# Ten projection units of a float32-by-halves kernel computed as seven block products instead of eight

## The chip, the cores and the metric

One core of a Trainium2 chip. The metric is the device time of one launch in microseconds. The three runs of the kernel before gave 1618.77, 1618.77 and 1618.57 us; the median is 1618.77 us.

## The reference, cut to what matters

A first block (three gated branches) and then a second one (S5, convolution, gated linear attention), all in float32, on 512 tokens of 1024 features. The change touches only the first block:

```python
h = rmsnorm(x, norm_g[l])
proj = jnp.einsum('bsd,dn->bsn', h, w_in[l])          # 512x1024 by 1024x12288
a_u, a_v, a_z, b_p, b_z, c_h, c_b, c_c, c_z, gate_logits = jnp.split(proj, SPLIT_OFFSETS, axis=-1)
yc = c_b * causal_depthwise_conv(c_c * c_h, conv_w[l], conv_b[l]) * jax.nn.silu(c_z)   # three taps
gates = jax.nn.sigmoid(gate_logits.reshape(bsz, s, N_BRANCH, D_MODEL))
merged = (gates[:, :, 0] * (ya @ w_branch_a) + gates[:, :, 1] * (yb @ w_branch_b)
          + gates[:, :, 2] * (yc @ w_branch_c))
x = x + merged @ w_out[l]
```

`g2` below is the third gate, `w_b` and `w_c` are the products with `w_branch_b` and `w_branch_c`.

## The kernel before, in words

**A unit.** Every projection of 1024 output columns is a section of two units of 512 columns. The activations lie transposed in SBUF, features on partitions, in eight tiles of 128 x 512. Each float32 operand is held as a sum of two reduced parts, HH + HL for the activations and WH + WL for the weights, and a product is three matmuls, high by high, high by low and low by high (`halves`, line 2418). A unit is therefore 8 feature tiles x 4 column tiles x 3 = 96 matmuls of 128x128 by 128x512, into the four PSUM banks of one half of PSUM; the next unit uses the other half. All of them are issued at line 2471 (function `unit` of the PE block, called by `section`).

**Weights.** A unit's weights come as four chunks of 128 x 1024 (512 KB). SP loads a chunk into one of four slots of WR (lines 524 to 558) as soon as the chunk four before it has been split (`w_lo`); ScalarE copies it to WH (line 999, `split`), which waits until PE has finished with the chunk four before (`weights_used`); VectorE subtracts, WL = WR - WH (line 1570); PE then waits for `w_lo`. A chunk is 24 matmuls.

**Order.** There is no planner. `JOBS` (lines 72 to 133) lists the units and side jobs in PE's order with how many PSUM evictions ScalarE (`a`) and VectorE (`d`) make for each, and every semaphore value is counted from it. Each engine's program is written out by hand in that order. Around the change PE runs g1, c_h, w_b, c_c, g2, c_b, c_z, w_c, w_out. ScalarE evicts g1, c_h, g2 and c_z (lines 1037 and 1051, four instructions a unit). VectorE multiplies c_c from PSUM onto CH (line 1850), makes the three taps (lines 1855 and 1861), multiplies c_b from PSUM (line 1871), multiplies by silu(c_z) from TMP (line 1624), splits the branch outputs into YH and YL (line 1607) and merges (`merge`, lines 1829 and 1831). The residual X (2 MB) and the row FROW (512 KB) are loaded by SP after c_h (lines 630 and 631).

Of the kernel before, what the change touches and what calls it, by code (L numbers as in the profile page):

```python
# [14 lines left out]
F32 = mybir.dt.float32  # L15
# [22 lines left out]
T4 = 4  # L38
# [42 lines left out]

_add("params", side=1, a=2)
# [147 lines left out]
def three_branch_s5_gla_kernel(nc, a, out):  # L230
    ctx = ExitStack()
    with ctx:
# [31 lines left out]
        TMP = put("TMP", "TMP", [2, NC])  # L264

# [117 lines left out]
        def bank(name, m):  # L383
# [30 lines left out]
        pool_g, pool_w, pool_t = sem("pool_g"), sem("pool_w"), sem("pool_t")  # L414
        pool_rep = sem("pool_rep")
# [32 lines left out]
            "xg_half", "x_sums", "x_base", "x_left", "x_sum"))  # L448
        halves_done, y2_half, yg_done = sem("halves_done"), sem("y2_half"), sem("yg_done")
# [60 lines left out]
        def _(sp):  # L510
# [50 lines left out]

            def x_tile(t):
                sp.dma_start(X[:, t, :], x_d[:, t, :]).then_inc(x_in[t], 16)
# [41 lines left out]
            sp.wait_ge(pool_g, 1)  # L605
# [21 lines left out]
            section("c_h", w_in, W_IN["c_h"])  # L627
            sp.wait_ge(side_done, side_after("pool.1"))
            sp.wait_ge(s5_out, 16 * S5_OUT)
            sp.dma_start(X[:, :, :], x_d).then_inc(x_again, 16)  # L630
            sp.dma_start(FROW[:, :], a["final_g"].rearrange("(o n) -> o n", o=1).broadcast_to([P, D])).then_inc(frow_in, 16)
            section("w_b", a["w_branch_b"][0], 0)
            for name in ("c_c", "g2", "c_b", "c_z"):
                section(name, w_in, W_IN[name])
            section("w_c", a["w_branch_c"][0], 0)
# [121 lines left out]
        def _(pool):  # L757
# [104 lines left out]
            pool.memset(MJ8[:, 0, 0:1], 0.0).then_inc(pool_w, 1)  # L862
# [20 lines left out]
            pool.memset(MJ8[:, 0, 1:2], 0.0).then_inc(pool_g, 1)  # L883
# [12 lines left out]
            pool.tensor_tensor(TM[:, :, :], TM[:, :, :], DT2[:, :, :], ALU.add).then_inc(pool_t, 1)  # L896

            pool.wait_ge(side_done, side_after("w_t.1"))
            for ri in range(2):
                pool.tensor_copy(WST[:, ri, :, 0:T4 - 1, :],  # L900
                                 WST[:, ri, :, T4 - 1:T4, :].to_broadcast([P, PAIRS, T4 - 1, S5_GROUP])).then_inc(pool_rep, 1)
# [81 lines left out]
        def _(act):  # L983
# [9 lines left out]
            def split(count=4):  # L993
# [8 lines left out]
                state["chunk"] = min(state["chunk"] + count, N_STATIC)  # L1002

# [136 lines left out]
            act.wait_ge(pool_t, 1)  # L1140
# [45 lines left out]
            evac("g1.0", [G[:, m, :] for m in range(4)], ACT.Sigmoid)  # L1186
            split()
# [1750 lines left out]
```

## Time and profile before

| what | value |
|---|---|
| median of the runs (1618.57 to 1618.77) | 1618.77 us |
| span of the profiled execution | 1617.1 us |
| what the median has beyond that span | 1.7 us |
| granted TensorE clock over the span | 0.999 |
| PE busy | 1606.0 us, 99% |
| VectorE busy | 952.0 us, 59% |
| ScalarE busy | 667.2 us, 41% |
| HBM traffic | 128 GB/s |

The profiled execution has no total of its own beside its span, so the working goes by the span and the 1.7 us are carried along. PE's busy time is the union of matmuls whose ends are modelled, so the share alone does not tell at what rate they follow each other; the distance between their starts does.

### The profile page before, as it was taken

What the parts mean: (1) busy time and instruction counts of PE and PEld (TensorE: products, weight loads), DVE (VectorE), ACT (ScalarE), POOL (GpSimd) and SP (SyncE); (2) the same over time, 40 slices, a digit from 0 to 9 for tenths busy, and PEclk for the clock granted to TensorE, in tenths of its full rate; (3) what the DMA queues carried; (4) which work ended last, traced back from release to release, by engine and by line L of the source; (5) the groups of instructions that cost most, each with busy time, mean ns of one, the idle gap of its engine ahead of it and who ended that gap; (6) DMA issues with size and microseconds to landing.
All of it is one profiled execution on the core that took longest, in us unless ns stands there. A gap on an engine that the chain in (4) does not pass through costs nothing.

```text
span 1617.1 us, 19917 instructions
## 1 busy us (share of the span) xinstructions
PE 1606.0 (99%) x7833; PEld 1344.3 (83%) x7833; DVE 952.0 (59%) x1325; ACT 667.2 (41%) x936; POOL 204.3 (13%) x237
## 2 busy tenths in 40 slices
PE   9999999999999999999999999999999999999998
PEld 7888888888888888888898889887888888888887
DVE  5267274663235424456899999985473535455357
ACT  5333342253222223335455454558255425343254
POOL 4991000000000000001323221121000000000000
PEclk9999999999999999999999999999999999999999
DMA  8664643233433333332988988498623123122221
GB/s 243 172 171 135 164 118 93 76 93 103 157 96 98 95 103 92 102 93 80 314 166 204 189 194 220 105 205 182 194 72 93 66 90 106 54 77 91 79 77 66
DMA packets 152395, 207.41 MB, mean 128 GB/s; under 512 B 52289, under 2 KB 75509, under 8 KB 151670
## 3 DMA queue, kind: packets, MB, share of 16 engines
q1 hardware_dynamic: 133077, 174.22, 34.9%
q0 software_dynamic: 17568, 29.89, 11.1%
q10 hardware_dynamic: 1664, 2.13, 0.5%
q8 instruction: 58, 0.95, 0.2%
q14 instruction: 28, 0.22, 0.0%
HBM read 191.53 MB, written 14.68 MB: 128 GB/s over the span
## 4 chain that ended last, share of the span: by engine, by line
PE 97%; DVE 1%; ACT 1%; DMA 0%; issue 0%; DVEq 0%; SPq 0%; ACTq 0%
PE PS L2471 82%; PE PS L2449 3%; PE PS L2839 1%; PE PS L2548 1%; PE PS L2789 1%; PE PS L2691 1%; PE PS L2869 1%; PE PS L2658 1%; PE PS L2641 0%; PE PS L2845 0%; PE PS L2717 0%; PE PS L2626 0%; PE PS L2715 0%; PE PS L2716 0%; ACT XN L1006 0%; PE PS L2826 0%
## 5 line engine op out<-in xcount | busy, mean ns | idle before, releaser
L2471 PE MATMUL PS<-HH,WH 128*128 128x512 f32 x1216 | 474.7, 390 | 0.8 <-ACT G L1037 0.4
L2471 PE MATMUL PS<-HH,WL 128*128 128x512 f32 x1216 | 473.3, 389 | 0.0
L2471 PE MATMUL PS<-HL,WH 128*128 128x512 f32 x1216 | 473.2, 389 | 0.0
L999 ACT ACTIVATE WH<-WR 128x1024 fp32r<-128x1024 f32 x200 | 211.9, 1061 | 596.9 <-PE PS L2471 558.9
L1570 DVE TENSOR_TENSOR WL<-WR,WH 128x1024 fp32r<-128x1024 f32 x144 | 186.1, 1299 | 391.9 <-ACT WH L999 391.3
L2471 PEld LDWEIGHTS PS<-HH,WH 128*128 128x128 f32 x1216 | 228.3, 188 | 49.4 <-issue 2.1
L2471 PEld LDWEIGHTS PS<-HH,WL 128*128 128x128 f32 x1216 | 228.3, 188 | 47.8
L2471 PEld LDWEIGHTS PS<-HL,WH 128*128 128x128 f32 x1216 | 228.3, 188 | 47.0
L2022 DVE SCALAR_TENSOR_TENSOR TMP<-CP,PRM,TMP 128x512 f32<-128x512 f32 x232 | 155.0, 748 | 0.0
L2471 PE MATMUL PS<-WH,HH 128*128 128x512 f32 x320 | 126.8, 396 | 0.0
L2471 PE MATMUL PS<-WL,HH 128*128 128x512 f32 x320 | 125.1, 391 | 0.0
L2471 PE MATMUL PS<-WH,HL 128*128 128x512 f32 x320 | 125.1, 391 | 0.0
L2471 PE MATMUL PS<-YH,WH 128*128 128x512 f32 x320 | 124.6, 389 | 0.0
L2471 PE MATMUL PS<-YH,WL 128*128 128x512 f32 x320 | 124.5, 389 | 0.0
L2471 PE MATMUL PS<-YL,WH 128*128 128x512 f32 x320 | 124.5, 389 | 0.0
L1601 DVE TENSOR_TENSOR WL<-WR,WH 128x1024 fp32r<-128x1024 f32 x64 | 76.3, 1220 | 52.5 <-ACT WH L1025 52.5
L1025 ACT ACTIVATE WH<-WR 128x1024 fp32r<-128x1024 f32 x64 | 66.3, 1058 | 83.0 <-PE PS L2471 81.8
L2471 PEld LDWEIGHTS PS<-WH,HH 128*128 128x128 f32 x320 | 67.9, 212 | 13.1 <-issue 3.0
L2471 PEld LDWEIGHTS PS<-WH,HL 128*128 128x128 f32 x320 | 67.9, 212 | 10.5 <-issue 0.7
L2471 PEld LDWEIGHTS PS<-WL,HH 128*128 128x128 f32 x320 | 67.9, 212 | 10.1
L2471 PEld LDWEIGHTS PS<-YL,WH 128*128 128x128 f32 x320 | 60.1, 188 | 12.5
L2471 PEld LDWEIGHTS PS<-YH,WH 128*128 128x128 f32 x320 | 60.1, 188 | 12.5
(398 smaller groups left out, 2099.6 us busy)
## 6 DMA issues: line engine op xcount, KB each, us to landing
WR<-in_w_in_dram SPq DMA_DIRECT2D x96, 512.0 KB, 3.8
WR<-in_od_w_in_dram SPq DMA_DIRECT2D x32, 512.0 KB, 4.0
WR<-in_ev_w_in_dram SPq DMA_DIRECT2D x24, 512.0 KB, 4.6
WL<-in_ev_w_in_dram POOLq DMA_DIRECT2D x24, 512.0 KB, 7.6
WR<-in_ev_w_in_dram SPq DMA_DIRECT2D x32, 256.0 KB, 3.1
WR<-in_ev_w_out_dram SPq DMA_DIRECT2D x16, 512.0 KB, 5.3
WR<-in_od_w_in_dram SPq DMA_DIRECT2D x32, 256.0 KB, 3.4
WR<-in_od_w_out_dram SPq DMA_DIRECT2D x16, 512.0 KB, 3.8
```

What stands on the lines that cost most here:

```text
L999: act.activation(WH[:, n % RING, :, :], WR[:, n % RING, :, :], ACT.Copy).then_inc(w_hi, 1)
L1025: act.activation(WH[:, j % RING, :, :], WR[:, j % RING, :, :], ACT.Copy).then_inc(w_hi, 1)
L1570: dve.tensor_tensor(WL[:, s, :, :], WR[:, s, :, :], WH[:, s, :, :].bitcast(F32), ALU.subtract).then_inc(w_lo, SUM_TO - SUM_FROM + 1 if n = ...
L1601: dve.tensor_tensor(WL[:, s, :, :], WR[:, s, :, :], WH[:, s, :, :].bitcast(F32), ALU.subtract).then_inc(w_lo, 1)
L2022: o = dve.scalar_tensor_tensor(CP[:, kt, CPAD:] if last else TMP[:, s, :], CP[:, kt, k:k + SEQ], w, TMP[:, s, :], ALU.mult, ALU.add)
L2449: mm = pe.matmul(out_banks[m], tok(acts(kt)[ai], m), (WH, WL)[wi][:, q, kk, :], start=(kt == 0 and i == 0), stop=(kt == KT - 1 and i == 2))
L2471: mm = pe.matmul(out_banks[m], st, mv, start=(kt == 0 and i == 0), stop=(kt == 2 * per - 1 and i == 2))
L2548: mm = pe.matmul(bank("a_v.0", t), tile(H(2 * q + kk)[ai], t), (WH, WL)[wi][:, q, kk, :], start=(q == 0 and kk == 0 and i == 0), stop=(q = ...
L2658: mm = pe.matmul(bank(f"pool.{i}", m), (PWH, PWL)[wi][:, g, k, (kt % 2) * P:(kt % 2 + 1) * P], Y(2 * g + k)[ai], start=(k == 0 and j == 0) ...
L2691: mm = pe.matmul(bank(f"s5_z.{i}", m)[:, r * P:(r + 1) * P], WT[m // 2][:, pr, :], UT[:, pr, :], start=True, stop=True)
L2789: mm = pe.matmul(out_bank[:, cols], tile(acts(kt)[ai], t), (WH, WL)[wi][:, 2 * u + kt // 2, kt % 2, cols], start=(kt == 0 and i == 0), sto ...
L2839: mm = pe.matmul(A[m][:, s * P:SEQ], (V2, V2L)[wi][:, s, m * P:(m + 1) * P], scores, start=(s == 0 and i == 0), stop=(s == TT - 1 and i == ...
```

## The change

Ten units (c_h, c_c, c_b, c_z and g2, two each) are computed by a seven-product scheme for 2 x 2 blocks (features halved, columns halved, tokens halved). A block product is 4 feature tiles x 2 column tiles x 3 = 24 matmuls of 128x128 by 128x256, so a unit is 168 of them. The activation side needs four combinations of blocks (S1 to S4), made once ahead of c_h. The weight side needs four sums of blocks for each unit, made on VectorE in place in the raw buffer. There are seven operands instead of four chunks to split for each unit, and the results are put together in SBUF by two ScalarE and five VectorE instructions. The products with silu and sigmoid are applied in place afterwards. The units of c_h and c_c now stand together, w_b comes after them, then c_b, c_z and g2; the taps of c run on VectorE under c_c.1 and w_b, the other elementwise work of c under c_b.1 to g2.1. The loads of X and FROW move behind g2.1. Some semaphores of POOL's tables are put together in one.

```diff
+def _seven(name, ends=(0, 0)):
+    for u in range(2):
+        SEVEN.append(f"{name}.{u}")
+        _add(f"{name}.{u}", 7 + ends[u], 0, 2, 5)
...
-_section("c_h", a=4)
+_seven("c_h")
+_seven("c_c")
 _section("w_b", d=4)
-_section("c_c", d=4)
-_section("g2", a=4)
-_section("c_b", d=4)
-_section("c_z", a=4)
+_seven("c_b")
+_seven("c_z")
+_seven("g2", (0, 2))
 _section("w_c", d=4)
...
+BLOCK_AT = ((0, 0), (0, 1), (1, 1), (1, 0))
+OPERAND_AT = (0, 0, 0, 1, 3, 2, 3)
+OPERAND_SUM = {1: 1, 3: 2, 2: 3, 6: 4}
... SP
+                for place in (1, 0, 2, 3) if again else range(4):
+                    if again and place == 0:
+                        sp.wait_ge(sums_made, sums_after(j - 1))
+                    elif again:
+                        sp.wait_ge(w_lo, chunks_before(before) + (0, 4, 6, 7)[place])
+                    else:
+                        sp.wait_ge(w_lo, n0 - RING + place + 1)
+                    i, half = BLOCK_AT[place]
+                    c0 = W_IN[name] + int(u) * NC + half * (NC // 2)
+                    sp.dma_start(WRS[:, place, :, :], w_in[4 * P * i:4 * P * (i + 1), c0:c0 + NC // 2]
...
+            sp.wait_ge(weights_used, used_after("g2.1"))
             sp.dma_start(X[:, :, :], x_d).then_inc(x_again, 16)
             sp.dma_start(FROW[:, :], ...)
... ScalarE
+            def high(job, i):
+                n, j = chunks_before(job) + i, SEVEN.index(job)
+                if i in OPERAND_SUM:
+                    act.wait_ge(sums_made, sums_after(j, OPERAND_SUM[i]))
+                else:
+                    act.wait_ge(w_loaded[OPERAND_AT[i]], 16 * block_loads(job))
+                act.wait_ge(weights_used, n - RING + 1)
+                act.activation(WHS[:, n % RING, :, :], WRS[:, OPERAND_AT[i], :, :], ACT.Copy).then_inc(w_hi, ends)
+            def seven(job, to, following, func=ACT.Copy, skip=0, acted=None, between=None):
+                def finish(i, j, k):
+                    if acted:
+                        act.wait_ge(banks_dve, dve_after(job, k))
+                        act.activation(block_of(to, i, j, kt0, skip), block_of(to, i, j, kt0, skip), func).then_inc(acted, 1)
+                act.wait_ge(weights_used, n0 + 1)
+                act.activation(block_of(to, 1, 1, kt0, skip), paired(job, 0), ACT.Copy).then_inc(banks_act, 1)
+                for i in range(4, 7):
+                    high(job, i)
+                if between:
+                    between()
+                next_high(following, 0)
+                act.wait_ge(weights_used, n0 + 5)
+                act.activation(block_of(to, 0, 0, kt0, skip), paired(job, 0), func).then_inc(banks_act, 1)
+                next_high(following, 1)
+                finish(1, 1, 3)
+                next_high(following, 2)
+                finish(0, 1, 4)
+                next_high(following, 3)
+                finish(1, 0, 5)
...
+            for i in range(3):
+                high("c_h.0", i)
+            act.wait_ge(weights_used, used_after("g1.1"))
+            combination_hi(4, corner(HH, 1, 0), S3R[:, :, :])
... VectorE
+            def low(job, i):
+                dve.wait_ge(w_hi, n + 1)
+                dve.tensor_tensor(WLS[:, n % RING, :, :], WRS[:, OPERAND_AT[i], :, :], WHS[:, n % RING, :, :].bitcast(F32),
+                                  ALU.subtract).then_inc(w_lo, ends)
+            def block_sum(to, other):
+                dve.tensor_tensor(WRS[:, to, :, :], WRS[:, to, :, :], WRS[:, other, :, :], ALU.add).then_inc(sums_made, 1)
+            def next_low(job, i):
+                low(job, i)
+                if i == 0:
+                    dve.wait_ge(w_loaded[1], 16 * block_loads(job))
+                    block_sum(0, 1)
+                elif i == 1:
+                    dve.wait_ge(sums_made, sums_after(j, 1))
+                    block_sum(0, 2)
+            def next_outer(job):
+                if job in SEVEN:
+                    dve.wait_ge(w_loaded[2], 16 * block_loads(job))
+                    block_sum(1, 2)
+            def seven(job, to, following, work=iter(()), paces=(1, 0, 1, 0, 1, 1), skip=0):
+                low(job, 4)
+                dve.wait_ge(sums_made, sums_after(j, 3))
+                block_sum(3, 0)
+                others(paces[0])
+                low(job, 5)
+                others(paces[1])
+                dve.wait_ge(banks_act, act_after(job, 1))
+                dve.wait_ge(weights_used, n0 + 3)
+                dve.tensor_tensor(c21, c22, c, ALU.subtract).then_inc(banks_dve, 1)
+                dve.wait_ge(banks_dve, dve_after(job, 1))
+                dve.tensor_tensor(c22, c21, b, ALU.add).then_inc(banks_dve, 1)
+                low(job, 6)
+                others(paces[2])
+                dve.wait_ge(weights_used, n0 + 4)
+                dve.scalar_tensor_tensor(c22, c22, -1.0, d, ALU.mult, ALU.subtract).then_inc(banks_dve, 1)
+                others(paces[3])
+                next_low(following, 0)
+                next_outer(following)
+                next_low(following, 1)
+                others(paces[4])
+                dve.wait_ge(weights_used, n0 + 6)
+                dve.scalar_tensor_tensor(c12, c21, -1.0, b, ALU.mult, ALU.subtract).then_inc(banks_dve, 1)
+                next_low(following, 2)
+                dve.wait_ge(weights_used, n0 + 7)
+                dve.tensor_tensor(c21, c21, d, ALU.add).then_inc(banks_dve, 1)
+                next_low(following, 3)
+                others(paces[5])
...
+            seven("c_c.0", U, "c_c.1")
+            seven("c_c.1", U, "w_b.0", taps, (1, 1, 1, 1, 1, 1))
+            for _ in taps:
+                pass
+            taps = convolved(1)
+            for n in (5, 5, 6):
+                split(1)
+                for _ in range(n):
+                    next(taps)
...
+            seven("c_b.1", CH, "c_z.0", weighed(0), skip=PPAD)
+            seven("c_z.0", CH, "c_z.1", weighed(1), skip=PPAD)
+            seven("c_z.1", CH, "g2.0", gated_c(0), skip=PPAD)
+            seven("g2.0", G, "g2.1", gated_c(1))
+            seven("g2.1", G, "w_c.0", low_c(range(4)))
... PE
+            def seven(job):
+                for i, (m, x) in enumerate(zip((0, 1, 2, 3, 0, 1, 3), blocks)):
+                    low_ready(n)
+                    if i < 4:
+                        free_bank(job, m)
+                    elif i == 4:
+                        pe.wait_ge(banks_act, act_after(job, 1))
+                    else:
+                        pe.wait_ge(banks_dve, dve_after(job, i - 3))
+                    if job == SEVEN[0] and 1 <= i < 4:
+                        pe.wait_ge(parts_dve, COMBINED + (1, 2, 4)[i - 1])
+                    for kt in range(4):
+                        for half in range(2):
+                            out_cols = slice(half * (SEQ // 2), (half + 1) * (SEQ // 2))
+                            for j, (wi, ai) in enumerate(halves):
+                                mm = pe.matmul(bank(job, m)[:, out_cols], (WHS, WLS)[wi][:, n % RING, kt, half * P:(half + 1) * P],
+                                               x[ai][:, kt, :], start=..., stop=..., skip_group_check=True)
+                    mm.then_inc(weights_used, used_after(job) - n if i == 6 else 1)
```

The four combinations take ten VectorE instructions of 128 x 1024 ahead of `next_low("c_h.0", 0)` (S1: three, S2: two, S4: two, S3: three, each waiting for the one before), four ScalarE copies to high parts, and four VectorE subtractions to low parts; the fourth pair overwrites a corner of HH and HL, so it waits for the end of g1.1.

## Rows read from the trace of the kernel before

**Rows 1.** The page: engines' busy time, and the granted clock.
```profile
PE 1606.0 (99%) x7833; PEld 1344.3 (83%) x7833; DVE 952.0 (59%) x1325; ACT 667.2 (41%) x936; POOL 204.3 (13%) x237
...
PEclk9999999999999999999999999999999999999999
```
**Rows 2.** Busy time by stretch: PE, PEld, DVE, ACT, POOL, PEclk, DMA share, GB/s.
```profile
450.00:620.00 170.00, 170.00 (x751) 140.81 (x751) 70.59 (x87) 36.77 (x39) 0.00 (x0) 1.00 0.33 96
...
990.00:1014.00 24.00, 24.00 (x213) 23.85 (x212) 24.00 (x38) 11.39 (x18) 1.20 (x1) 1.00 0.87 263
```
**Rows 3.** Who waited for whom, 300 to 760 us.
```profile
ACT WH L999 <- PE PS L2471: 281.4, 72, 4.4
...
PEld PS L2519 <- DVE XN L1910: 0.3, 1, 0.3
```
**Rows 4.** Timeline of PE in a unit: first and last of 75 512-column matmuls.
```profile
1354.77 0.39 PE L2471 MATMUL PS<-HH,WH 128*128 128x512 f32 x1
...
1371.54 0.39 PE L2471 MATMUL PS<-HH,WL 128*128 128x512 f32 x1
```
**Rows 5.** Timeline near the end: first and last of 24 256-column matmuls, one load.
```profile
1608.56 0.28 PE L2789 MATMUL PS<-WH,OH 128*128 128x256 f32 x1
1608.57 0.19 PEld L2789 LDWEIGHTS PS<-WH,OL 128*128 128x128 f32 x1
...
1611.32 0.28 PE L2789 MATMUL PS<-WL,OH 128*128 128x256 f32 x1
```
**Rows 6.** Chain of waits: pairs of 128-column matmuls, each with its weight load.
```profile
991.27 0.22 PE PS L2716 x2
991.49 0.22 PE PS L2717 x2
```
**Rows 7.** Groups by line and shape, VectorE and ScalarE, 320 to 760 us.
```profile
L1570 DVE TENSOR_TENSOR WL<-WR,WH 128x1024 fp32r<-128x1024 f32 x79 | 96.3, 1224 | 224.6 <-ACT WH L999 224.6
...
L1829 DVE TENSOR_TENSOR TMP<-PS,G 128x512 f32<-128x512 f32 x16 | 10.9, 683 | 0.0
...
L999 ACT ACTIVATE WH<-WR 128x1024 fp32r<-128x1024 f32 x77 | 81.5, 1060 | 263.9 <-PE PS L2471 263.9
```
**Rows 8.** Timeline of VectorE: runs of instructions, and one that waits for another.
```profile
361.50 4.91 DVE L1607 TENSOR_TENSOR YL<-CH,YH 128x512 fp32r<-128x512 f32 x8
366.32 2.35 DVE L1570 TENSOR_TENSOR WL<-WR,WH 128x1024 fp32r<-128x1024 f32 x2
...
378.19 1.23 DVE L1570 TENSOR_TENSOR WL<-WR,WH 128x1024 fp32r<-128x1024 f32 x1 [4.21 <-ACT WH L999]
...
466.37 0.68 DVE L1829 TENSOR_TENSOR TMP<-PS,G 128x512 f32<-128x512 f32 x1
467.09 0.69 DVE L1831 TENSOR_TENSOR M<-M,TMP 128x512 f32<-128x512 f32 x1
...
514.11 5.38 DVE L1861 SCALAR_TENSOR_TENSOR U<-CH,PRM,U 128x512 f32<-128x512 f32 x8
```
**Rows 9.** Timeline of ScalarE: splits, a table load and an eviction around g1.
```profile
371.66 1.06 ACT L999 ACTIVATE WH<-WR 128x1024 fp32r<-128x1024 f32 x1 [4.38 <-PE PS L2471]
...
378.18 1.28 ACT L1037 ACT_TABLE_LOAD   x1
379.47 2.07 ACT L1037 ACTIVATE G<-PS 128x512 f32<-128x512 f32 x4
```
**Rows 10.** DMA issues: KB each, median us to landing.
```profile
WR<-in_w_in_dram SPq DMA_DIRECT2D x96, 512.0 KB, 3.8
...
WR<-in_ev_w_in_dram SPq DMA_DIRECT2D x32, 256.0 KB, 3.1
...
X<-in_x_dram SPq DMA_DIRECT2D x1, 2048.0 KB, 8.7
...
FROW<-in_final_g_dram SPq DMA_DIRECT2D x1, 512.0 KB, 9.5
```

More of the change, by code:

```diff
@@ L626, in _ @@
             section("g1", w_in, W_IN["g1"])
-            section("c_h", w_in, W_IN["c_h"])
-            sp.wait_ge(side_done, side_after("pool.1"))
-            sp.wait_ge(s5_out, 16 * S5_OUT)
+            for job in SEVEN[0:4]:
+                blocks(job)
+            sp.wait_ge(sums_made, sums_after(3))
+            section("w_b", a["w_branch_b"][0], 0)
+            for job in SEVEN[4:]:
+                blocks(job)
+            sp.wait_ge(sums_made, sums_after(len(SEVEN) - 1))
+            section("w_c", a["w_branch_c"][0], 0)
+            sp.wait_ge(weights_used, used_after("g2.1"))
             sp.dma_start(X[:, :, :], x_d).then_inc(x_again, 16)
             sp.dma_start(FROW[:, :], a["final_g"].rearrange("(o n) -> o n", o=1).broadcast_to([P, D])).then_inc(frow_in, 16)
[L632 to L635, printed above, removed]
             section("w_out", a["w_out"][0], 0)
@@ L1210, in _, with combination_hi @@
[L1210 to L1214 removed]
+            def combination_hi(k, hi, raw):
+                act.wait_ge(parts_dve, k)
+                act.activation(hi, raw, ACT.Copy).then_inc(parts_act, 1)
+            combination_hi(1, S1H[:, :, :], S1R[:, :, :])
+            combination_hi(2, S2H[:, :, :], S2R[:, :, :])
@@ new lines, in _ @@
+            combination_hi(3, S4H[:, :, :], S4R[:, :, :])
+            for i in range(3):
+                high("c_h.0", i)
+            act.wait_ge(weights_used, used_after("g1.1"))
+            combination_hi(4, corner(HH, 1, 0), S3R[:, :, :])
+            high("c_h.0", 3)
+            evac("g1.1", [G[:, 4 + m, :] for m in range(4)], ACT.Sigmoid)
+            act.wait_ge(y_lo, 24)
+            seven("c_h.0", CH, "c_h.1", skip=PPAD)
+            seven("c_h.1", CH, "c_c.0", skip=PPAD)
+            act.wait_ge(parts_dve, 2 * COMBINED)
@@ new lines, in _ @@
+            seven("c_c.0", U, "c_c.1")
+            seven("c_c.1", U, "w_b.0")
+            split()
+            for i in range(4):
+                high("c_b.0", i)
+            act.wait_ge(parts_dve, taps_after(0))
+            seven("c_b.0", CH, "c_b.1", skip=PPAD)
+            act.wait_ge(parts_dve, taps_after(1))
+            seven("c_b.1", CH, "c_z.0", skip=PPAD)
+            act.wait_ge(parts_dve, weighed_after(0))
+            seven("c_z.0", CH, "c_z.1", ACT.Silu, PPAD, parts_act)
+            act.wait_ge(parts_dve, weighed_after(1))
@@ new lines, in _ @@
+            seven("c_z.1", CH, "g2.0", ACT.Silu, PPAD, parts_act)
+            act.wait_ge(weights_used, used_after("w_b.1"))
+            act.wait_ge(banks_dve, dve_after("w_b.1"))
+            seven("g2.0", G, "g2.1", ACT.Sigmoid, acted=parts_act, between=lambda: y_halves(
+                tmp_free, lambda kt: 8 + kt + 1, lambda kt: U[:, kt, :], range(4)))
+            seven("g2.1", G, "w_c.0", ACT.Sigmoid, acted=parts_act, between=lambda: y_halves(
+                tmp_free, lambda kt: 8 + kt + 1, lambda kt: U[:, kt, :], range(4, 8)))
```

265 lines of the change are left out of this document (182 added, 83 removed).

## The prediction

> **What bounds the kernel now.** I read the page first. PE is busy in 99% of the span and the clock is granted in full throughout [rows 1]. A modelled busy share says little about pace, so the next view is the stretch that the change rewrites: in 450 to 620 us PE is busy without a gap, VectorE in 42% and ScalarE in 22% of the time [rows 2]. The waits from 300 to 760 us say who sets that: ScalarE waited 281 us for PE to give slots back, and of waits by PE's queues only 0.3 us at one place are found, a weight load ahead of the second block [rows 3]. So PE's instruction stream is the time here, and the helpers have slack. What counts is then the distance between starts of matmuls, read from the timelines. 75 matmuls of 512 columns start from 1354.77 to 1371.54 us: 16.77 / 74 = 0.2266 us each [rows 4]. 24 of 256 columns start from 1608.56 to 1611.32 us: 2.76 / 23 = 0.1200 us each, every one with a weight load of its own [rows 5]. Half the columns cost 53% of the time: there is a fixed part of about 0.013 us in each.
>
> **The sum on PE.** A unit before is 96 x 0.2266 = 21.75 us. After it is 168 x 0.1200 = 20.16 us. The gain is 1.59 us a unit, 15.9 us in ten units, though an eighth of the columns (2.7 us a unit) has gone: 1.1 us of it is eaten by 72 more starts. The break-even distance is 21.75 / 168 = 0.1295 us. Below the rows at 0.1200 the nearest limit is that of weight loads: in the stage of 128-column matmuls a pair of them takes 0.22 us, so one load with its matmul 0.111 us [rows 6], and 24 us of that stage ran at full busy [rows 2], which is a long stretch, so feeding instructions that fast is possible. 0.111 lies under 0.1200, so the columns should still decide, with 8% to spare. Reading errors of 0.01 us at both ends of the 24 make 0.0004 us on the distance, 0.7 us on the sum.
>
> The Trainium skill, "TensorE: Matmul & The Clock Gate", section "Back-to-back issue gap", gives isolated gaps of 518 cycles for 512 columns and 262 for 256, nearly without a fixed part; by it the gain would be some 24 us (my estimate). The rows say 0.2266 and 0.1200 and decide.
>
> **What VectorE gets.** Its instructions overlap a little: eight of 512 columns take 4.91 us, (4.91 - 0.68) / 7 = 0.60 us apart; two of 1024 take 2.35 us against 1.22 for one, so 1.13 us apart; eight three-operand ones (5.38 - 0.74) / 7 = 0.66 us apart; one that waits for its predecessor starts 0.72 us after it instead of 0.60 [rows 8]. A block sum and a low part are both 128 x 1024, taken as the low part of before, 1.22 us long [rows 7]. A unit now has 7 low parts and 4 sums (11 x 1.13 = 12.4 us), three results at 0.60 and two at 0.66 (3.1 us): 15.5 us, plus some 0.5 us where one waits for the other. Units that carry branch work have four multiplications or low parts more (2.4 us), c_c.1 six instructions of c's taps (4 x 0.60, and two at most 0.60: up to 3.6 us). That makes 16 to 19.6 us under a unit of 20.16 us. Covered, but from 42% busy to 80 to 97%: the cover is thin now. Evictions removed on VectorE (c_c, c_b) come back as multiplications in SBUF of the same length [rows 7]. The other ten taps of c_c.0 and the sixteen of c_c.1 lie under w_b's 43.5 us.
>
> The Trainium skill, "VectorE: DVE Perf Modes", section "The DRAIN you can't avoid", says that the next instruction starts only when the pipe has emptied. Rows 8 speak against it in full (0.60 apart, 0.68 long), and by it the sum would be that of the second case below.
>
> **ScalarE.** Seven high parts of 1.06 us, two evictions (four took 2.07 us, so about 0.5 each), for c_z and g2 three in place, for g2 four YH parts of at most 1.06 more [rows 7, 9]: 8.4 to 14.2 us of 20.16, and a table load of 1.28 us more than before (silu, then sigmoid, where sigmoid was there from g1). Covered. Its part in c_h.0 is the one that can be late (below).
>
> **The order inside a unit**, start = 0, products ending every 2.88 us. VectorE makes low 4 by 5.7 (ScalarE evicts product 0 at 2.9 and copies operand 4 by 4.5), the fourth sum by 6.9, low 5 by 8.1, waits for product 2, makes two results by 10.1 and low 6 by 11.2. It waits for product 3 (11.5), then third result, low 0 of the next unit, two sums, low 1, third sum by about 18.5, fourth result, low 2 by 20.9, last result, low 3 by some 23.7. PE wants the next unit's operands 0 to 3 at 20.2, 23.0, 25.9 and 28.8, so the smallest lead is about 3.5 us. Products 5 and 6 wait for results, made by 10.1 and 12.3, wanted at 14.4 and 17.3.
>
> **The start, c_h.0.** This is the thinnest place. VectorE ends the last split of g1 at 379.4 us [rows 8]. Ten dependent instructions of 1.26 us (1.22 and a wait) bring it to 392; three low parts of combinations to 395.4; low 0 of c_h.0 at 396.6; two sums; high 1 on ScalarE, low 1 at 400.1; sum; high 2, low 2 at 403.6; fourth combination's low part; low 3 at 405.9. g1.1 ends at 398.6: a split at 371.66 follows the third chunk of g1.0, and five chunks of 5.44 us come after it (24 matmuls; also 4.21 idle and 1.23 busy between splits) [rows 8, 9]. PE wants low 1 at 401.5, low 2 at 404.4, low 3 at 407.2. All are met, with 0.8 us at low 2; VectorE then stays about 1 us ahead to the start of c_h.1 and catches up behind it. I allow 0.4 us of stall for these places; the bounds are 0 and, with each instruction lasting its full 1.22 us without overlap, 1.5 us.
>
> **The end, w_c.** The dummy counts at the end of g2.1 hold the second chunk of w_c back until its last product; low 1 comes 2.3 us after it and is wanted 5.44 us after it. The YL tiles 3 to 7 are written 7 to 10 us after it, tile 3 wanted at 8, tile 4 at 10.9: tight, no stall. Before, the work of c_z lay here, now it lies a section earlier.
>
> **DMA and SP.** The bytes are the same: four blocks of 512 KB a unit. Rows are 1 KB instead of 2 KB; the nearest rows with 1 KB pieces are pairs of 256 KB, 3.1 us to landing against 3.8 us for 512 KB [rows 10]: 3.8 to 5 us for a block. The next unit's place 0 can be issued only after the fourth sum (6.9) and is wanted at 11.5: 4.6 us. X and FROW (8.7 and 9.5 us [rows 10]) leave the queue ahead of w_b and stand ahead of w_out's chunks, which are wanted some 27 us later; X itself is wanted 65 us after g2.1. POOL's part is a renamed semaphore. Nothing.
>
> **The sum.** 1617.1 - 15.9 + 0.4 = 1601.6 us of span, and the 1.7 us that the median has beyond the span: 1603.3 us.
>
> **The rivals.**
> (1) Forecast, 0.78: PE's distance decides, stalls up to 1.5 us: 1602.2 to 1604.4 with the reading error.
> (2) VectorE's hand-offs eat part of it, 0.13. For: 80 to 97% load, and every block sum sits between a high and a low part of two engines. Without any overlap the loss is 1.5 us, almost all of it in c_h. If sums in place or strided results cost 0.2 us more than the rows (15% more, an estimate), a unit with branch work needs 18 to 22 us; the start loses 20 instructions x 0.2 less its lead of 0.8, some 3 us, c_c.1 up to 2 us, and units near 20 us up to 4 us in their hand-offs: 5 to 9 us, so 1608 to 1612.
> (3) Slower, 0.05: the raw blocks land late. Place 0 of a unit waits for the last sum of the one before, and from its landing to that unit's last sum lie two high parts (2.2 us with waits), five low parts (0 to 4, 5.7), four sums (4.7) and two results (1.3), about 14 us and half a microsecond of waits. The loop is 14.5 us + the landing. It fits in 20.16 us up to 5.7 us of landing and costs a microsecond a unit for each one beyond; at 7.3 us the whole gain is gone, at 8.5 us the kernel is 12 us slower, 1631. Against: 3.8 and 3.1 us [rows 10], DMA a third busy [rows 2].
> (4) The distance of 0.1200 us does not hold for long, since weight loads come within 8% of it, 0.04: at 0.125 the gain is 7.5 us (1611), at 0.1295 none; counted half as faster, half as the same or slower. A weight load of 0.19 us [rows 5] at its full length a matmul would give 1719, but the rows show them overlapping.
>
> A measurement of this kernel can tell 0.2%, 3.2 us, from no change. Faster by more: case 1, nearly all of 2, half of 4: 0.93. Slower: most of 3 and a little of 4: 0.04. The same: 0.03. The range 1601.5 to 1609 holds case 1 with the reading error on both sides and the nearer half of case 2.
>
> **What would show it.** In the profile after: 1680 matmuls of 256 columns, starts 0.120 us apart, first product of c_h.1 20.2 us after that of c_h.0; VectorE at 75 to 95% between 400 and 480 and 520 to 645 us; no wait of PE for VectorE over 1 us except perhaps in c_h.0 and at c_h.1; w_c starting near 644 instead of 660 us. I am wrong if the distance is over 0.122, if PE's waits for WLS add up to more than 2 us, or if raw blocks land later than 5.7 us and ScalarE waits for them.

## The result: 20.1 us less, and the profile after

The kernel after takes 1598.62 us (1598.18 to 1598.64), beside 1618.72 us for the kernel before in the same runs. The ratio is 0.9875, with a 95% interval of 0.9861 to 0.9889. That is 20.1 us less. The prediction was 1603.3 us, 15.5 us less, with a range of 1601.5 to 1609: the direction and what bounds the kernel were right, one price was wrong, and the time lies 2.9 us below the range. The span of the profiled execution fell from 1617.1 to 1596.8 us, by 20.3, at the same granted clock of 0.999.

The page of the kernel after, engines' busy time (before: [rows 1]):

```profile
PE 1585.8 (99%) x8553; PEld 1361.4 (85%) x8553; DVE 1077.9 (68%) x1459; ACT 708.5 (44%) x979; POOL 204.2 (13%) x237
```

PE has 720 matmuls more (10 x 168 against 10 x 96) and is busy 20 us less. VectorE has 126 us more to do and nobody pays for it, which the next views have to confirm.

Busy time by stretch of the kernel after (PE, PEld, DVE, ACT, POOL, granted clock, DMA share, GB/s), over c_h and c_c, w_b, and c_b to g2:

```profile
400.00:480.00 80.00, 80.00 (x673) 79.51 (x673) 67.84 (x71) 38.28 (x43) 0.00 (x0) 1.00 0.40 123
480.00:520.00 40.00, 40.00 (x178) 33.10 (x178) 32.75 (x45) 7.43 (x7) 0.00 (x0) 1.00 0.23 72
520.00:645.00 125.00, 125.00 (x1040) 123.81 (x1039) 108.82 (x121) 65.15 (x78) 0.30 (x1) 1.00 0.36 110
```

PE has no gap in any of the three. VectorE stands at 85, 82 and 87%, where it stood at 42% before [rows 2].

All waits of PE in the kernel after, over the whole span:

```profile
PE PS L2863 <- POOL MJ L870: 2.5, 1, 2.5
PE PS L2840 <- DVE XN L1873: 0.6, 1, 0.6
PE PS L3009 <- ACT AS L1420: 0.5, 1, 0.5
PE PS L2752 <- DVE WL L1824: 0.4, 1, 0.4
PE PS L2774 <- ACT G L1176: 0.4, 1, 0.4
PE PS L2774 <- DMA WL<-in_ev_w_in_dram: 0.4, 1, 0.4
PE PS L2774 <- ACT TMP L1190: 0.3, 1, 0.3
PE PS L2851 <- DVE HL L1863: 0.2, 1, 0.2
```

They sum to 5.3 us (before 5.4), and the line of the seven products, L2987, is not among them: PE never waits in the ten units. The one wait without a like before is that for the WL loaded ahead of the second block's weights, 0.4 us.

What remains is the distance between starts. The timeline of PE in c_h.0 of the kernel after, at the borders of the first products (start, length, instruction):

```profile
401.13 0.28 PE L2987 MATMUL PS<-HH,WLS 128*128 128x256 f32 x1
401.25 0.29 PE L2987 MATMUL PS<-S1H,WHS 128*128 128x256 f32 x1
...
403.88 0.28 PE L2987 MATMUL PS<-S1H,WLS 128*128 128x256 f32 x1
403.99 0.28 PE L2987 MATMUL PS<-S2H,WHS 128*128 128x256 f32 x1
...
406.71 0.28 PE L2987 MATMUL PS<-HH,WHS 128*128 128x256 f32 x1
...
412.45 0.29 PE L2987 MATMUL PS<-S4H,WHS 128*128 128x256 f32 x1
...
415.19 0.28 PE L2987 MATMUL PS<-HH,WHS 128*128 128x256 f32 x1
...
420.81 0.28 PE L2987 MATMUL PS<-HH,WLS 128*128 128x256 f32 x1
420.93 0.29 PE L2987 MATMUL PS<-S1H,WHS 128*128 128x256 f32 x1
```

Products are 24 matmuls, numbered 0 to 6 in a unit. Those that read a corner (one of the four blocks) of HH and HL come two in a row: 406.71 to 412.45 is 5.74 / 48 = 0.1196 us a matmul, 415.19 to 420.93 the same. The product that reads S1 takes 403.99 - 401.25 = 2.74 / 24 = 0.1142, S2 2.72 / 24 = 0.1133, S4 2.74 / 24 = 0.1142. All have the same form, 128x128 by 128x256, and the same modelled length, so neither the group means nor the busy share tell them apart; only starts do.

These are means over whole products. Inside them only two steady distances are found, 0.1200 us for corners and 0.1133 us for S tiles, and a short passage where the tile changes. The ninth matmul of product 3 and the first of product 4 show it:

```profile
407.65 0.28 PE L2987 MATMUL PS<-HH,WLS 128*128 128x256 f32 x1
...
409.57 0.28 PE L2987 MATMUL PS<-HH,WHS 128*128 128x256 f32 x1
```

The first eight of product 3, right behind S2, are 0.94 / 8 = 0.1175 us apart and the other sixteen 1.92 / 16 = 0.1200. So the corner products behind an S product (3 and 6) have a mean of 0.1192, those behind another corner product (4, and 0 of most units) 0.1200. S1 and S4, behind a corner, lose 0.02 us in their first three matmuls: that is why S2 alone shows 0.1133. From product 1 of c_h.0 to product 1 of c_h.1 it is 420.93 - 401.25 = 19.68 us, where 20.16 was forecast and 21.75 was the time before. All ten units show it alike, so the ten gain 20.7 us: c_h.0 starts at 398.38 us instead of 398.60 (the early waits for XN and HL are 0.5 us shorter in this execution), and w_c starts 21.0 us earlier, at 638.71 instead of 659.72:

```profile
638.59 0.28 PE L2987 MATMUL PS<-HH,WLS 128*128 128x256 f32 x1
638.71 0.40 PE L2774 MATMUL PS<-YH,WH 128*128 128x512 f32 x1
```

By the scan of the second block (970.9 us after, 991.1 before) 20.2 us are left; 0.4 of the 0.8 lost in between is the wait for WL above. From there to the end it stays within 0.1 us.

### The profile page after: what moved, and what is told of

Same layout as the page of the kernel before. It is cut to its first block, busy times and chain, and to the rows that moved or that the text cites. A ratio compares the mean times of both kernels' runs of the same rounds, so it can differ in the third digit from the quotient of the medians.

```text
span 1596.8 us, 21474 instructions
## 1 busy us (share of the span) xinstructions
PE 1585.8 (99%) x8553; PEld 1361.4 (85%) x8553; DVE 1077.9 (68%) x1459; ACT 708.5 (44%) x979; POOL 204.2 (13%) x237
## 4 chain that ended last, share of the span: by engine, by line
PE 94%; DMA 2%; DVE 2%; ACT 1%; issue 0%; SPq 0%; DVEq 0%; ACTq 0%
PE PS L2774 67%; PE PS L2987 12%; PE PS L2752 3%; PE PS L3168 1%; PE PS L2851 1%; DMA WR<-in_ev_w_in_dram 1%; PE PS L3118 1%; PE PS L3020 1%; PE PS L3198 1%; PE PS L2961 1%; DMA WL<-in_ev_w_in_dram 1%; PE PS L2944 0%; PE PS L3174 0%; PE PS L3045 0%; PE PS L2929 0%; PE PS L3046 0%
## 5 line engine op out<-in xcount | busy, mean ns | idle before, releaser
L2774 PE MATMUL PS<-HH,WH 128*128 128x512 f32 x896 | 350.2, 391 | 0.8 <-ACT G L1176 0.4
L2774 PE MATMUL PS<-HH,WL 128*128 128x512 f32 x896 | 348.8, 389 | 0.0
L2774 PE MATMUL PS<-HL,WH 128*128 128x512 f32 x896 | 348.7, 389 | 0.0
L2774 PEld LDWEIGHTS PS<-HH,WH 128*128 128x128 f32 x896 | 168.2, 188 | 37.3 <-issue 2.1
L2774 PEld LDWEIGHTS PS<-HH,WL 128*128 128x128 f32 x896 | 168.2, 188 | 35.3
L1109 ACT ACTIVATE WHS<-WRS 128x1024 fp32r<-128x1024 f32 x70 | 73.8, 1060 | 93.2 <-DVE WRS L1736 38.1
L1730 DVE TENSOR_TENSOR WLS<-WRS,WHS 128x1024 fp32r<-128x1024 f32 x70 | 85.3, 1221 | 23.9 <-ACT WHS L1109 23.9
L2987 PE MATMUL PS<-HH,WLS 128*128 128x256 f32 x320 | 90.5, 283 | 0.0
L2987 PE MATMUL PS<-HH,WHS 128*128 128x256 f32 x320 | 90.4, 283 | 0.0
L2987 PE MATMUL PS<-HL,WHS 128*128 128x256 f32 x320 | 90.3, 282 | 0.0
```

The lines of the kernel that those rows point to most:

```text
L1109: act.activation(WHS[:, n % RING, :, :], WRS[:, OPERAND_AT[i], :, :], ACT.Copy).then_inc(w_hi, ends)
L1730: dve.tensor_tensor(WLS[:, n % RING, :, :], WRS[:, OPERAND_AT[i], :, :], WHS[:, n % RING, :, :].bitcast(F32), ALU.subtract).then_inc(w_lo, ...
L2774: mm = pe.matmul(out_banks[m], st, mv, start=(kt == 0 and i == 0), stop=(kt == 2 * per - 1 and i == 2))
L2987: mm = pe.matmul(bank(job, m)[:, out_cols], (WHS, WLS)[wi][:, n % RING, kt, half * P:(half + 1) * P], x[ai][:, kt, :], start=(i < 4 and kt ...
```

## The experiments

Times are the slowest core's; the kernel before, run beside each set, gave 1619.39, 1618.72 and 1619.07 us, so sets agree within 0.7 us. e5, e9 and e12 have four runs, the others one. A "distance" is the mean distance between starts of matmuls over a product or a stretch, read from timelines as above.

**e1: which property of the tiles makes the pace.** Corner rows lie 2048 bytes apart, rows of S tiles 1024; corners alternate between HH and HL.

```diff
+S1X = put("S1X", "R3", [4, SEQ], F32R)
+S1H = S1X[:, :, 0:SEQ // 2]
+S1L = S1X[:, :, SEQ // 2:SEQ]
...
-blocks = [(corner(HH, 0, 0), corner(HL, 0, 0)), (S1H, S1L), ...
-          (corner(HH, 0, 1), corner(HL, 0, 1)), (S4H, S4L), (corner(HH, 1, 1), corner(HL, 1, 1))]
+blocks = [(dense(HH), dense(HL)), (S1H, S1L), ...
+          (corner(HH, 0, 1), corner(HH, 0, 1)), (S4H, S4L), (S1H, S1L)]
```

> The change's block products have two distances between starts: 0.1196 us where the moving tile is a corner of HH and HL (products 0, 3, 4, 6), 0.1133 us where it is S1, S2 or S4 (products 1, 2, 5). This kernel reads other places of SBUF in four of the seven products (so the results of the ten units are not the reference's): product 0 reads 4 x 256 of HH and HL without gaps between feature tiles; S1's high and low part lie interleaved in one tile, so product 1 steps 2048 bytes from feature tile to feature tile like a corner of HH; product 4 reads the high part HH in all three matmuls; product 6 reads S1 into bank 3. Row-distance theory: product 0 goes to 0.113, product 1 and 6 to 0.120. Place theory (where the moving tile lies in SBUF decides): products 0 and 4 stay at 0.120, product 1 and 6 at 0.113. Bank theory (banks 1 and 2 are fast, 0 and 3 slow): nothing changes, 6 stays at 0.120. Alternation theory (switching between high and low tile 16384 bytes apart costs): only product 4 goes to 0.113. Time: within 3 us of 1598.6.

Measured: 1596.8 us. HH and HL read densely 0.1192 (behind an S product), S1 read with the corner's row distance 0.1141, HH alone 0.1200, S1 in product 6's bank 0.1133. The pace goes with the tile, not with row distance, bank or alternation. The unit is 0.16 us shorter by its starts (0.14 in product 6, 0.02 in the product behind it), 1.6 us in ten units, and 1.8 were measured.

**e2: pairs that mix tiles.**

```diff
-blocks = [(corner(HH, 0, 0), corner(HL, 0, 0)), (S1H, S1L), (S2H, S2L), (corner(HH, 1, 0), corner(HL, 1, 0)),
-          (corner(HH, 0, 1), corner(HL, 0, 1)), (S4H, S4L), (corner(HH, 1, 1), corner(HL, 1, 1))]
+blocks = [(corner(HH, 0, 0), corner(HL, 0, 0)), (corner(HH, 0, 1), corner(HL, 0, 1)), (S2H, corner(HL, 0, 0)),
+          (corner(HH, 1, 0), S1L), (S1H, S1L), (S4H, S4H), (S4H, S1L)]
```

> Other operands in products 1 to 6 (results not the reference's): product 1 (bank 1) reads a corner of HH and HL; product 2 reads S2's high part and a corner of HL; product 3 a corner of HH and S1's low part; product 4 (bank 0) reads S1; product 5 reads S4's high part in all three matmuls; product 6 (bank 3) S4's high and S1's low part. Place theory: 1 at 0.120, 4, 5 and 6 at 0.113, products 2 and 3 in between (2 nearer to 0.113, since two of three matmuls read S2, 3 nearer to 0.120). Bank theory: products 1, 2 and 5 at 0.113 and 3, 4, 6 at 0.120 as before. Alternation theory: 1 at 0.120, 5 at 0.113, 2 and 3 slow.

Measured: 1597.5 us. Product 1 from corners 0.1200; S2H with a corner of HL 0.1179; a corner of HH with S1L 0.1179; S1, behind the mixed product, 0.1142; S4H alone and S4H with S1L 0.1133. The pace goes with the tiles wherever the product stands in the unit. A mixed product lies between the two paces, but not by its shares, as I had expected: one reads S tiles in two matmuls of three, the other in one of three, and both have the same distance.

**e3: the whole of SBUF's allocation 64 bytes further.**

```diff
-start = nc.sbuf_base + -nc.sbuf_base % 32
+start = nc.sbuf_base + -nc.sbuf_base % 32 + 64
```

> The whole arena begins 64 bytes later; nothing else. HH, HL, WH and WL then begin at 64 and the S tiles at 0 on a grid of 128 bytes, the reverse of the change. If the begin on that grid decides, corner products go to 0.113 (and 512-column matmuls perhaps from 0.2267 to 0.220, which would take up to 40 us off the kernel), S products to 0.120: the ten units take 0.9 us longer or shorter by their mix (four products of seven become faster, three slower: 1.5 us shorter in ten units). If the region, the row distance, the bank or the alternation decides: no difference, 1598.6 us within 1 us.

Measured: 1598.4 us, all distances as in the kernel after (0.2269 for 512 columns, 0.1196 corners, 0.1142, 0.1133, 0.1142). A shift common to all tiles doesn't matter on this scale.

**e4: 64 bytes between the weight tiles and everything else.**

```diff
-("WL", 16384), ("HH", 16384)
+("WL", 16384), ("pad", 64), ("HH", 16384)
```

> A pad of 64 bytes between WL and HH: HH and HL begin at 64 on the grid of 128 bytes, the S tiles at 0, the weights stay at 0. Theory that moving and stationary tile must differ on the grid: corner products 0.113, S products 0.120. Theory of the moving tile's own begin: the same here, but with e3 also 0.113 and 0.120, where the relative theory has e3 unchanged. Region, row distance, bank or alternation: no difference.

Measured: 1619.3 us, 20.7 more than the kernel after, from 64 unused bytes. It is no wait: PE is still busy without a gap from 400 to 520 and 520 to 645 us. The first and the last matmul of stretches of g1, the kernel after and then this one:

```profile
383.64 0.39 PE L2774 MATMUL PS<-HL,WH 128*128 128x512 f32 x1
...
394.98 0.39 PE L2774 MATMUL PS<-HH,WH 128*128 128x512 f32 x1
```

```profile
383.65 0.39 PE L2774 MATMUL PS<-HH,WL 128*128 128x512 f32 x1
...
394.87 0.39 PE L2774 MATMUL PS<-HH,WH 128*128 128x512 f32 x1
```

The first holds 51 matmuls, 11.34 / 50 = 0.2268 us apart; the second 50, 11.22 / 49 = 0.2290 apart, and where weights are the moving tile it is 0.234. Corners fell to 0.1179, not to the 0.1133 that one theory had; S products, whose tiles now start on a multiple of 1024 bytes from WH as HH's did, rose to 0.1200. With e3 this says that places of tiles relative to each other set the pace, though not which pair of tiles it is. The same 64 bytes made the corner products faster and the 512-column matmuls slower.

One product of this run goes further. Product 0 of c_b.0, behind w_b, and product 0 of c_b.1, behind a corner product, each from its first matmul to the first of product 1:

```profile
526.21 0.28 PE L2987 MATMUL PS<-HH,WHS 128*128 128x256 f32 x1
...
528.93 0.28 PE L2987 MATMUL PS<-S1H,WHS 128*128 128x256 f32 x1
```

```profile
546.06 0.28 PE L2987 MATMUL PS<-HH,WHS 128*128 128x256 f32 x1
...
548.89 0.29 PE L2987 MATMUL PS<-S1H,WHS 128*128 128x256 f32 x1
```

The first is 2.72 / 24 = 0.1133 us a matmul, the second 2.83 / 24 = 0.1179, as in the other eight units. Both read the same corner, at the same address, and product 0 of c_h.0 and of g2.0 even takes its weights from the same slot as that of c_b.0. So the places of the tiles alone do not fix the pace. What I find different is what ran before, and that this holds the pace for a whole product is an inference.

**e5 and e6: R1 (17344 bytes) between WL and HH**, in the kernel after and in the kernel before. It moves HH by 960 bytes past a multiple of 16384, which is where the S tiles stood.

```diff
-("WL", 16384), ("HH", 16384), ("HL", 16384), ("YH", 16384), ("YL", 16384), ("R1", 17344), ("R2", 16384)
+("WL", 16384), ("R1", 17344), ("HH", 16384), ("HL", 16384), ("YH", 16384), ("YL", 16384), ("R2", 16384)
```

> Only the order of the SBUF regions changes: R1 (17344 bytes, 16384 + 960) lies between WL and HH. HH, HL, YH and YL then begin 960 bytes past a multiple of 16384 from WH, as the S tiles do already; R1 itself (V, CH, CP, QK) moves to 0. Relative-place theory (the distance between starts depends on how the moving tile lies to the stationary tile, modulo 1024 bytes or more): corner products go from 0.1196 to 0.1133 us, S products stay at 0.1133; ten units gain 96 x 0.0063 x 10 = 6 us. 512-column matmuls may follow, from 0.2267 to 0.220; if they do, the kernel gains some 35 us more. Theory that S tiles are fast for another reason than this distance (their region of SBUF): corner products stay at 0.1196, 1598.6 us.

> The kernel before the change, with the same move of R1. Relative-place theory: its 512-column matmuls have the same distance as those of e5; if that is 0.220, the kernel before gains 30 to 45 us and the change is worth (96 x 0.220 - 168 x 0.1133) x 10 = 21 us on it, as on the old layout. If 512-column matmuls do not follow, 1618.7 us within 2 us.

Measured: 1626.44 us (1626.09 to 1626.72), ratio to the kernel before 1.0046 with an interval of 1.0029 to 1.0063, and 1653.5 us for the kernel before in this layout. I had expected corners at 0.1133 and thought 0.220 possible for 512 columns; they came at 0.1178 and 0.2334. The S tiles and the weights did not move, and yet all S products, from their first matmul to their last, came at 0.1178. So an address rule for each product by itself is refuted. The change is worth 27.1 us on this layout, where 21 had been expected, since its gain is counted from matmuls of 0.2334: by distances it is (96 x 0.2334 - 168 x 0.1178) x 10 = 26.2.

**e7: 128 bytes instead of 64.**

```diff
-("WL", 16384), ("HH", 16384)
+("WL", 16384), ("pad", 128), ("HH", 16384)
```

> A pad of 128 bytes between WL and HH: HH and HL lie at +128 from WH modulo 1024, the S tiles at 960 + 128 = 1088, so +64. With e4, HH at +64 had 0.1179 us and the S tiles at 0 had 0.1200. Relative-place theory: the S products now have what HH had at +64, 0.118; HH at +128 is unknown, between 0.113 and 0.120; 512-column matmuls were 0.2286 in e4 and are slower than 0.2267 again or the same. If only HH's and S's own tiles mattered, S would stay at 0.120 or go back to 0.1133.

Measured: 1629.9 us; 512 columns 0.2331, corners 0.1186, S products 0.1178. The S tiles stand here as far from the weights, but for multiples of 1024, as HH stood in e4, and have its pace of 0.1179: that part of the expectation held. It proves little, since e5 shows the same 0.1178 with S tiles that did not move.

**e8: two low parts more on VectorE in each unit**, to take its cover away (EXTRA = 2).

```diff
+n = n0 + 4
+dve.wait_ge(w_hi, n + 1)
+for _ in range(EXTRA):
+    seq.inc(dve.tensor_tensor(WLS[:, n % RING, :, :], WRS[:, OPERAND_AT[4], :, :],
+                              WHS[:, n % RING, :, :].bitcast(F32), ALU.subtract))
+    seq.wait()
 low(job, 4)
```

> Two subtractions of 128 x 1024 more on VectorE in each of the ten units, ahead of low part 4, each waited for (2 x 1.26 us); results unchanged. Forecast's reading (VectorE is covered, 16 to 19 us of work in a unit, and the unit is now 19.7 us): the spare of about 4 us in plain units takes them, units with branch work (six) run over by 0.5 to 2 us: 5 to 12 us slower than the change, 1604 to 1611. If VectorE's work is not on the path at all, below 1 us; if VectorE already sets the pace, the full 25 us.

Measured: 1610.9 us, 12.3 more than the kernel after. The waits of PE on the line of the seven products (L2994 here), and the stretch of c_z and g2:

```profile
PE PS L2994 <- DVE CH L1785: 3.4, 4, 1.2
PE PS L2994 <- DVE WLS L1731: 3.2, 4, 1.2
PE PS L2994 <- DVE G L1785: 2.3, 2, 1.2
```

```profile
596.00:636.00 40.00, 36.78 (x309) 36.21 (x308) 39.44 (x43) 21.29 (x28) 0.00 (x0) 1.00 0.30 93
```

VectorE is at 99% and PE has gaps for the first time: this is what rival 2 would have looked like in the kernel after, and none of it is there. The loss lies just above the 5 to 12 expected, and the starts of the ten units account for all of it.

**e9: all seven products read corners of HH and HL.**

```diff
-blocks = [..., (S1H, S1L), (S2H, S2L), ..., (S4H, S4L), ...]
+blocks = [..., (corner(HH, 0, 1), corner(HL, 0, 1)), (corner(HH, 1, 1), corner(HL, 1, 1)), ...,
+          (corner(HH, 0, 0), corner(HL, 0, 0)), ...]
```

> All seven products of every unit read corners of HH and HL, none an S tile (so the ten units are not the reference's; the S tiles are still made). Theory: the 72 matmuls a unit that read S tiles run 0.0063 us closer together than the 96 that read corners, and that alone is what the forecast missed. Then every product has 0.1196 to 0.1200 us, a unit 20.1 to 20.2 us, and the kernel 10 x 72 x 0.006 = 4.3 to 4.8 us more than the change: 1603.0 to 1603.6, the forecast's number. Rival, that the ten units gain for another reason (less time in gaps, or a later stage is shorter): 1598.6.

Measured: 1603.45 us (1602.68 to 1604.36), ratio to the kernel before 0.9905 with an interval of 0.9888 to 0.9921: 4.8 us more than the kernel after, and the forecast's number within 0.2 us. PE's timeline of products 1 and 2 of c_h.0 in this kernel:

```profile
401.27 0.28 PE L2989 MATMUL PS<-HH,WLS 128*128 128x256 f32 x1
...
407.15 0.28 PE L2989 MATMUL PS<-HH,WHS 128*128 128x256 f32 x1
```

That is 5.88 us for 49 steps, 0.1200 each, with no break where the S tiles were read. All ten units take 20.15 or 20.16 us, as forecast for the kernel after. The missing term is therefore the pace of the S products, and with it the miss is explained but for some tenths; the four runs of e9 lie 1.7 us apart, so that the medians agree within 0.2 us is in part luck.

**e10: 64 bytes ahead of R6 alone, where S4 lies.**

```diff
-("R5", 16384), ("R6", 8192)
+("R5", 16384), ("pad", 64), ("R6", 8192)
```

> A pad of 64 bytes between R5 and R6: only S4's high and low part (and small tables behind them) move, from 960 to 1024 past a multiple of 16384 from WH. Relative-place theory, by what S did in e4: product 5 goes from 0.1142 to 0.120 us, the six others stay; ten units lose 24 x 0.006 x 10 = 1.4 us: 1600.0. If S tiles were slow in e4 only because HH had moved too, product 5 stays at 0.1142 and the time at 1598.6.

Measured: 1601.3 us. PE's timeline of product 5 of c_h.0, this kernel's first and last matmul (the kernel after: 412.45 to 415.08 for the same 24):

```profile
412.06 0.28 PE L2987 MATMUL PS<-S4H,WHS 128*128 128x256 f32 x1
...
414.82 0.28 PE L2987 MATMUL PS<-S4H,WLS 128*128 128x256 f32 x1
```

2.76 / 23 = 0.1200, and S1, S2 and corner products 0, 3 and 4 keep their distances. Product 6, whose corner did not move either, went from 0.1192 to 0.1200, because the fast matmuls ahead of it are gone. Moving one tile changed the pace of the product that reads it. The unit is 0.16 us longer, 1.6 us in ten. The total is 1.2 us over what was expected; PE's waits add up to 2.0 us more in other places (the longest one for HL of 1.1 us, 0.2 in the kernel after), which one run doesn't explain.

**e11: R1 between HL and YH**, so that only YH, YL and R1 move.

```diff
-("HL", 16384), ("YH", 16384), ("YL", 16384), ("R1", 17344), ("R2", 16384)
+("HL", 16384), ("R1", 17344), ("YH", 16384), ("YL", 16384), ("R2", 16384)
```

> R1 lies between HL and YH: HH, HL, the weights and the S tiles are all where the change has them, YH and YL are moved by 960 as in e5. e5 had the S products at 0.1179 with the S tiles and the weights at the change's own addresses. If the tile read in the product decides alone, S products stay at 0.1133 here and e5's 0.1179 has to come from HH's products around them (the pace is handed on from product to product); w_b and w_c, which read YH and YL, go from 0.2268 to about 0.232. If R1's own place (the evictions into CH) slows PE, S products are at 0.1179 here too. Time: the stages that read YH and YL are some 3500 matmuls at most, so 3 to 15 us more than the change.

Measured: 1604.5 us. All seven products keep the pace of the kernel after, and 512 columns from YH and YL take 0.2333 instead of 0.2267. Moving R1, YH and YL therefore isn't what slowed the S products in e5. What e5 moved besides, and the units read, is HH and HL. That points to the products around them handing their pace on, as w_b may have done to one product in e4; it was not tried.

**e12: one low part more in each unit** (e8's edit with EXTRA = 1).

> One subtraction of 128 x 1024 more on VectorE in each of the ten units (1.26 us), as e8 with one instead of two. e8 lost 12.3 us of 25. By the schedule of the forecast, now with 19.7 us a unit, one more fits in every unit but c_c.1 and the start of c_h: 0 to 1.5 us more than the change, 1598.6 to 1600.1. If VectorE already set the pace, e8's loss would be linear: 6 us for one, 1604.7.

Measured: 1602.92 us (1601.46 to 1603.71), ratio to the kernel before 0.9902 with an interval of 0.9886 to 0.9919: 4.3 us more than the kernel after. The expectation of 0 to 1.5 was wrong; the loss is nearer to the 6 of a VectorE that already sets the pace. Waits of PE on the line of the seven products, and where one falls, in c_z:

```profile
PE PS L2994 <- DVE CH L1785: 1.6, 2, 1.1
```

```profile
596.38 0.36 PE L2994 MATMUL PS<-S4H,WHS 128*128 128x256 f32 x1 [1.06 <-DVE CH L1785]
```

One instruction of 1.22 us in a unit of 19.68 us already makes the S4 product (product 5) wait for a result. The kernel after has that result ready 0.5 us ahead of product 5 in c_h.0 (which starts at 412.45), 1.5 in c_b.0 and 3.3 to 4.1 in the others:

```profile
411.22 0.69 DVE L1778 TENSOR_TENSOR CH<-CH,PS 128x512 f32<-128x512 f32 x1
```

VectorE is busy for up to 19.1 of a unit's 19.68 us there (c_b.1), so one instruction more leaves a delay that grows from unit to unit: in e12 the result comes 12.8, 14.2 and 15.2 us after the start of c_b.1, c_z.0 and c_z.1, where it came at 10.5, 10.7 and 10.8. By their starts the ten units take 3.2 us more in the profiled execution, of which 1.6 are the waits above; that execution was the fastest of the four (1601.46), and the median lies 1.5 us above it, so the rest varies between runs.

## Why the prediction was wrong by 4.7 us, and where it was right

**What bounds the kernel: right.** The distance between starts on PE is the time; it alone gives 20.7 us of gain up to w_c, of which 20.3 are left in the span, and no other engine appears among PE's waits in the ten units.

**The sum on PE: here the prediction failed.** "After it is 168 x 0.1200 = 20.16 us" took one distance, from 24 matmuls near the end of the kernel [rows 5], for all 168, and "Reading errors of 0.01 us at both ends of the 24" stood as its only bound. Of the 168, 96 read corners and take 0.1196, 72 read S tiles and take (0.1142 + 0.1133 + 0.1142) / 3 = 0.1139: 11.48 + 8.20 = 19.68 us. The term was oversized by 0.48 us a unit, 4.8 us in ten, as e9 shows by taking exactly this away: 1603.45 us. For the corners the price was right, 0.1200 once they run steadily. For the S tiles it was not, and with it fell "a fixed part of about 0.013 us in each": 2 x 0.1133 = 0.2266 us, the distance for 512 columns, so two matmuls of 256 columns from S tiles cost no more than one of 512. The span of 1601.6 us forecast, less 4.8, less the 0.4 allowed for stalls, less the 0.2 by which c_h.0 started early, plus 0.7 lost again behind w_c, is 1596.9; 1596.8 were measured. The 256-column rows were alike in shape and data type, but read other tiles, with the roles changed too: there WH and WL are the moving tiles and OH and OL the stationary ones. The lower limit of 0.111 from weight loads [rows 6] had been named, and should have been the end of the range for tiles that no row showed; with 0.111 for the 72 the range would have reached down by 72 x 0.009 x 10 = 6.5 us. No rival had a shorter distance, and the sign of being wrong looked above 0.122 only. Two smaller slips did not decide it: an error of 0.01 us at both ends of the 24 makes 0.0009 us on the distance and 1.5 us on the sum, not 0.0004 and 0.7; and "an eighth of the columns (2.7 us a unit)" counts the fixed part among the columns, by the prediction's own figures it is 2.6, and 1.0 is eaten.

**The start, c_h.0: right, and a little too careful.** The timeline of VectorE in the kernel after, low parts 1 and 2 of c_h.0:

```profile
398.34 1.23 DVE L1730 TENSOR_TENSOR WLS<-WRS,WHS 128x1024 fp32r<-128x1024 f32 x1
401.82 1.23 DVE L1730 TENSOR_TENSOR WLS<-WRS,WHS 128x1024 fp32r<-128x1024 f32 x1 [1.13 <-ACT WHS L1109]
```

Low 1 ends at 399.6 (forecast 400.1), low 2 at 403.05 (403.6), and PE starts product 2 at 403.99. The 0.4 us allowed for stalls was not taken.

**VectorE's work: right on the sum, too easy on its cover.** 82 to 87% busy lies in the forecast's 80 to 97%. The order inside a unit came as written: the two results "by 10.1" end 10.0 to 10.8 us after the start of eight of the ten units. But that schedule is for a unit that starts without delay. In c_h.0 and c_b.0 the results came at 13.5 and 12.6 us, and the lead ahead of the S4 product, 4.3 us by the schedule, was 0.5 and 1.5. That is what runs out first, as e12 shows with one instruction and e8 with two (4.3 and 12.3 us).

**ScalarE, the end, and DMA: right.** Groups and waits of the kernel after, 320 to 740 and 396 to 645 us, and its DMA issues:

```profile
L1730 DVE TENSOR_TENSOR WLS<-WRS,WHS 128x1024 fp32r<-128x1024 f32 x70 | 85.3, 1221 | 23.9 <-ACT WHS L1109 23.9
L1736 DVE TENSOR_TENSOR WRS<-WRS 128x1024 f32<-128x1024 f32 x40 | 47.9, 1218 | 0.0
```

```profile
DVE WLS L1730 <- ACT WHS L1109: 23.9, 20, 4.2
ACT WHS L1109 <- DMA WRS<-in_w_in_dram: 9.1, 4, 2.6
```

```profile
WRS<-in_w_in_dram SPq DMA_DIRECT2D x40, 512.0 KB, 3.6
```

Sums in place cost 1.22 us like a low part, as taken. Raw blocks land in 3.6 us with their 1 KB rows, below the 3.8 to 5 forecast; ScalarE waits for them four times, 9.1 us in all, and PE never feels it. The YL tiles after g2.1 cause no wait of PE in w_c.

**The rivals.** VectorE's hand-offs (2) need waits of PE for CH, G or WLS written by VectorE, and the kernel after has none in the ten units. Late raw blocks (3) needed a landing above 5.7 us. A distance that does not hold (4) fell the other way: it is shorter, and the same in all ten units.

**What stays open.** Why the place of a tile changes the pace. Shown are: in one layout the tile decides and not its row distance, bank or order (e1, e2); its place relative to other tiles, and not a common shift of all by 64 bytes (e3, e4); 64 bytes in front of one tile change the pace of the product that reads it (e10); the pace of S products changed without any move of theirs when HH moved (e5); one corner product ran at 0.1133 behind w_b and at 0.1179 everywhere else (e4). So the places of the tiles that a matmul reads do not fix its pace alone. For 256 columns the same three distances return, 0.1133, 0.1177 to 0.1179 and 0.1200, except for the corners of e7 (0.1186). No rule that I formed from this forecast all of it: the same offset of 960 bytes goes with 0.1133 (kernel after) and with 0.1178 (e5) for 256 columns, and with 0.2334 for 512 (e5). No layout tried was faster than the kernel after by more than 0.3 us.

## What to carry to other kernels

Where PE is the bound, take the distance between starts from rows that read the same tiles as well as the same shape; where the new matmuls read tiles of their own, no row gives their price, and the range has to reach to the nearest limit on the other side (here from 0.1200 down to 0.111). When a layout of SBUF is touched in such a kernel, compare start distances of untouched matmuls before and after, since a move of 64 bytes can outweigh the edit. A schedule made by hand holds for the unit in which it starts without delay; ask for the lead of results and evictions also in the first unit and in those behind other work, and whether a helper's busy time leaves room to catch up.

## What the runs showed of the hardware that I had not expected

Matmuls with a weight load each follow each other at a pace that depends on where the moving tile lies relative to the others: 256 columns at 0.1133 to 0.1200 us, 512 columns at 0.2267 to 0.234 us, at a granted clock of 1.00 in the stretches read. For this kernel 64 unused bytes cost 20.7 us (e4), and moving one region 28 us with the change and 35 us without it (e5, e6). None of it shows in busy shares, in waits or in the modelled duration of a 256-column matmul, which is 0.27 to 0.29 us at any of these distances. At its shortest, 0.1133 us for 256 columns lies close to the 0.112 us between the 128-column matmuls at 971 us, which also have a weight load each. On VectorE a sum written in place was no slower than a low part written into another tile (1.22 us each).
